# The samples' attention moved half a unit back in TensorE's order, in one layer of a hybrid decoder

## The chip, the cores and the metric

The kernel runs on one core of one Trainium2 chip. The time is the device time of one execution in microseconds (us); a change is judged by the median of several executions. The profile is that of one execution, whose times are counted from the start of its span.

## The reference

One step of a one-layer decoder is computed, in float32, for two kinds of rows at once: a prompt of 512 tokens and 8 samples of one token each, 520 columns in all. Cut to what matters:

```
h = modulate(rms_norm(x, g_pre_mix), shift_m, scale_m)
u, q, k, v, z_pool, z_att = split(h @ w_in)
y_pool = pool_mix(u_ext, pos, w_map, scale) @ w_proj_pool
# samples: 24 heads = 3 groups x 8 slots, 129 keys each, 128 of them from a cache
s = einsum('btsd,btjsd->btsj', q, kg) * HEAD_DIM ** -0.5
p = exp(s - m);  o = einsum('btsj,btjsd->btsd', p, vg) / den
o = merge_groups(outs, lses)            # 3 groups -> 8 slots of 64
y_att = o @ w_proj_att
mix = (sigmoid(z_pool) * y_pool + sigmoid(z_att) * y_att) @ w_out
x = x + gate_m * rms_norm(mix, g_post_mix)
...                                     # then a convolved, gated feed-forward
```

The new key and value caches are outputs too, so that large copies in HBM run beside the computation.

## The kernel before

Activations lie transposed in SBUF: 128 channels on the partitions, 520 columns (TC) beside each other, D = 1024 as 8 such tiles. A product with a weight matrix is cut into **units**. A full unit has 8 weight tiles of 128x128 (512 KB), loaded by SP into one of four `raw` buffers. ScalarE copies it to `w_hi` in a rounded format (L699, in its helper `split`), VectorE takes the rest, `w_lo` (L932, in its own `split`), and TensorE multiplies in `blocks` (L1335) hi by hi, hi by lo and lo by hi: 24 groups of two matmuls for each output tile, one group for each weight tile loaded. A unit's result is in one of two PSUM accumulators, and `take` waits until the one needed has been evacuated. The splits of a unit are done two units ahead.

Each engine has its own program, written out by hand in a fixed order, and they meet in semaphores. The change is in the **middle stage**, whose order is `MID`: two units `map`, eight units `pp` (the projection of the pooled branch), four units `pa` (the projection of the attention, two output tiles each, from `o_hi` and `o_lo`). The `out` units come behind it. Within a `pp` unit TensorE does four tiles, then whatever was put in the middle, then the other four.

The attention of the samples is threaded through this stage in steps:

- GpSimd multiplies cached keys by queries (L672); VectorE sums each product over the head's channels in six reductions, `sample_scores(0)` to `sample_scores(5)` (L1139, output `sall`). The last is issued in the iteration of `pp` 4, behind that iteration's weight split.
- `sample_in` (TensorE, L1609): three transposes that sort the scores so that each of the 64 pairs of sample and slot has a partition. It waits for all six reductions.
- `sample_softmax` (VectorE, L1143 to L1161, with ScalarE's exponential at L818 in the middle), which also makes `o_new`, the part of the new token.
- `sample_turn` (TensorE, L1615): three transposes of the softmax weights into PSUM; VectorE copies them to `prT` (L1192, three copies).
- `sample_values` (TensorE, L1627): 48 matmuls of `prT` with the cached values `vS`, which SP loads in six blocks (`load_v`, 1 MB each). Before `load_v(5)` SP waits for the sixth reduction.
- VectorE adds `o_new` and masks, giving `o_rows` (L1198, L1201).
- `sample_out` (TensorE, L1635): eight small matmuls that put each head of a pair of slots and each sample in its place, as columns 512 to 519 of the attention's output.
- ScalarE and VectorE write these columns as `o_hi` and `o_lo` (L829, L1209, semaphore `os_lod`).

The first attention unit, pa0, is done in quarters by `one_half` (L1344): two output tiles, each with the first 260 columns (half 0) and then the last 260 (half 1). Only half 1 has the samples' columns, so TensorE waits for `os_lod` between the halves.

On VectorE, an iteration of `pp` holds in this order: what the samples need, the product of `thp` with the accumulator (L1206, which frees it), the split of the weights two units ahead, and a reduction of scores. SP's order of transfers around here is: pp6's tile, two V blocks, pp7's tile, two V blocks, pa0's tile, V blocks 4 and 5, the tiles of pa1 to pa3, some small outputs, the tiles of `out`. With the first `out` units go the loads `ada_last` (1 MB each), the first of which waits until `sample_values` is done.

Of the kernel before, what the change touches and what calls it, by code (L numbers as in the profile page):

```python
# [8 lines left out]
ALU = mybir.AluOpType  # L9
# [90 lines left out]
def program(nc, ins, outs):  # L100
# [5 lines left out]
    with ExitStack() as ctx:  # L106
# [582 lines left out]
        def _(act):  # L689
# [108 lines left out]
            for pos, (what, m) in enumerate(MID):  # L798
# [17 lines left out]
                if (what, m) == ("pp", 5):  # L816
                    act.wait_ge(smp_max, 1)
                    act.activation(sc[0:NB * NS, :], sc[0:NB * NS, :], ACT.Exp, bias=bh_stat[0:NB * NS, 0:1], scale=1.0,  # L818
                                   accum_out=bh_stat[0:NB * NS, 1:2]).then_inc(smp_exp, 1)
# [7 lines left out]
                if (what, m) == ("pp", 7):  # L827
                    act.wait_ge(smp_summed, 1)
                    act.activation(o_hi[:, :, TP:TC], psT[:, 0:PAIRS * NB].rearrange("p (a b) -> p a b", a=PAIRS), ACT.Copy).then_inc(os_hid, 1)  # L829
# [84 lines left out]
        def _(dve):  # L914
# [256 lines left out]
            for pos, (what, m) in enumerate(MID):  # L1171
# [12 lines left out]
                if what == "pp":  # L1184
                    if m == 5:
                        sample_softmax()
                    if m == 7:
# [6 lines left out]

                        dve.wait_ge(pv_done, 1)
# [7 lines left out]

                    done(dve, u)
                    v = halves(thp[:, m, :])
                    dve.scalar_tensor_tensor(v, v, 1.0, of(("pp", m)), ALU.add, ALU.mult).then_inc(free(("pp", m)), 1)  # L1206
                    if m == 7:
                        dve.wait_ge(os_hid, 1)
                        dve.tensor_tensor(o_lo[:, :, TP:TC], psT[:, 0:PAIRS * NB].rearrange("p (a b) -> p a b", a=PAIRS),  # L1209
                                          o_hi[:, :, TP:TC].bitcast(F32), ALU.subtract).then_inc(os_lod, 1)  # L1210
                    split(N[u] + 2)
                    if m < 5:
                        sample_scores(m + 1)
                    if m == 7:
                        dve.wait_ge(ada_out, OADA)
                        gains(gg_m, 0, KT, 16, 56, 0.0)
# [111 lines left out]
        def _(pe):  # L1328
# [310 lines left out]
            for pos, (what, m) in enumerate(MID):  # L1639
# [13 lines left out]
                if what == "pp":  # L1653
# [4 lines left out]
                    if m == 5:  # L1658
                        sample_in()
                    if m == 7:  # L1660
                        sample_values()
# [6 lines left out]
                    if m == 6:  # L1668
                        sample_turn()
                    if m == 7:  # L1670
                        sample_out()
                if what == "pa":
                    if m == 0:

                        for q in range(2):
                            take(("pa", q))
                            one_half(("pa", q), slot, [(2 * kt + q, kt) for kt in range(4)], o_hi, o_lo, 0)
                        pe.wait_ge(os_lod, 1)
# [147 lines left out]
```

## Time and profile before

| | |
|---|---|
| median of 3 runs | 1068.6 us (1068.44 to 1069.54) |
| the profiled execution, its own time | 1067.55 us |
| its span | 1065.7 us |
| TensorE busy | 1023.8 us, 96% of the span |
| VectorE, ScalarE, GpSimd busy | 480.4, 401.7, 120.3 us |
| mean granted clock of TensorE | 0.975 of full speed |
| middle stage | about 469 to 571 us |

The engines are named PE (TensorE), DVE (VectorE), ACT (ScalarE), POOL (GpSimd) and SP; SPq is SP's queue of transfers, and PEld are TensorE's weight loads. L12 is line 12 of the kernel. The granted clock is 1.00 at 2.4 GHz. A row of a timeline gives the start, how long it took, engine, line, output and inputs, how many instructions it merges, and in brackets the engine's idle time before it with what ended it. Matmuls are pipelined, so that one that takes 0.40 us by its row is followed by the next after 0.24; starts are what to count by.

### The profile page before, as it was taken

How to read it: one execution, taken by the hardware profiler on the slowest of the kernel's cores; microseconds unless marked ns; L12 is line 12 of the kernel's file. 1: busy time of each engine (PE TensorE's matmuls, PEld its weight loads, DVE VectorE, ACT ScalarE, POOL GpSimd, SP SyncE). 2: the span in 40 equal slices, each digit the busy share in tenths (PEclk: the TensorE clock that was granted, in tenths of full speed). 3: DMA queues.
4: the chain of work that ended last, by engine and by line, in shares of the span. 5: the costliest groups of instructions: out<-in, count | busy, mean ns of one | idle time of the engine just before them, and what ended most of it. 6: DMA issues, size and time to landing. Idle time of an engine off the chain costs nothing.

```text
span 1065.7 us, 20398 instructions
## 1 busy us (share of the span) xinstructions
PE 1023.8 (96%) x8597; PEld 969.5 (91%) x8597; DVE 480.4 (45%) x861; ACT 401.7 (38%) x642; POOL 120.3 (11%) x165
## 2 busy tenths in 40 slices
PE   5999999999999999999899987999999999999995
PEld 3799999999999999998889965999999999999994
DVE  6533324331443143338846356556555565422214
ACT  5424422433244224432114345444545545322213
POOL 1000300040004000416512021000000000000000
PEclk8899999999999999999999997999999999999996
DMA  9966676667666876329967670566666666665302
GB/s 315 284 210 206 208 236 237 214 207 245 235 211 206 260 251 231 121 75 379 366 220 234 195 234 35 167 228 214 229 221 221 228 218 200 198 218 177 106 25 81
DMA packets 227721, 222.30 MB, mean 209 GB/s; under 512 B 6270, under 2 KB 191998, under 8 KB 226846
## 3 DMA queue, kind: packets, MB, share of 16 engines
q1 hardware_dynamic: 227545, 220.85, 62.8%
q8 instruction: 69, 1.13, 0.5%
q14 instruction: 23, 0.18, 0.0%
q10 hardware_dynamic: 84, 0.15, 0.0%
HBM read 213.56 MB, written 96.03 MB: 291 GB/s over the span
## 4 chain that ended last, share of the span: by engine, by line
PE 87%; DVE 5%; ACT 2%; DMA 2%; SPq 1%; issue 1%; POOL 1%; ACTq 0%; POOLq 0%; DVEq 0%
PE acc L1335 75%; PE psS L1507 2%; PE psT L1521 2%; DMA raw<-in_w_proj_pool 1%; PE psS L1495 1%; DMA ada_first<-in_w_ada 1%; PE psT L1535 1%; POOL ssq L638 1%; DVE w_lo L932 1%; DVE xT L1274 1%; PE psT L1555 1%; PE psS L1493 1%; PE acc L1601 1%; ACT norm_u L728 1%; PE psS L1387 1%
## 5 line engine op out<-in xcount | busy, mean ns | idle before, releaser
L1335 PE MATMUL acc<-act_hi,w_hi 128*128 128x260 f32 x1920 | 395.3, 287 | 7.4 <-DVE act_lo L1005 5.0
L1335 PE MATMUL acc<-act_hi,w_lo 128*128 128x260 f32 x1920 | 387.7, 284 | 0.0
L1335 PE MATMUL acc<-act_lo,w_hi 128*128 128x260 f32 x1920 | 387.4, 283 | 0.0
L932 DVE TENSOR_TENSOR w_lo<-raw,w_hi 128x1024 fp32r<-128x1024 f32 (+1 forms) x148 | 190.1, 1285 | 357.8 <-ACT w_hi L699 357.2
L1335 PEld LDWEIGHTS acc<-act_hi,w_hi 128*128 128x128 f32 x1920 | 297.3, 190 | 16.1 <-DVE act_lo L1005 7.8
L1335 PEld LDWEIGHTS acc<-act_hi,w_lo 128*128 128x128 f32 x1920 | 297.0, 189 | 0.0
L1335 PEld LDWEIGHTS acc<-act_lo,w_hi 128*128 128x128 f32 x1920 | 297.0, 189 | 0.0
L699 ACT ACTIVATE w_hi<-raw 128x1024 fp32r<-128x1024 f32 (+1 forms) x148 | 154.9, 1046 | 180.3 <-PE acc L1335 170.1
L1335 PE MATMUL acc<-g_hi,w_hi 128*128 128x260 f32 x352 | 71.0, 283 | 0.0
L1335 PE MATMUL acc<-g_hi,w_lo 128*128 128x260 f32 x352 | 70.8, 282 | 0.0
L1335 PE MATMUL acc<-g_lo,w_hi 128*128 128x260 f32 x352 | 70.6, 282 | 0.0
L882 ACT ACTIVATE he<-acc 128x520 f32<-128x520 f32 x44 | 26.7, 607 | 87.6 <-PE acc L1335 87.6
L1335 PEld LDWEIGHTS acc<-g_lo,w_hi 128*128 128x128 f32 x352 | 54.3, 188 | 0.0
L1335 PEld LDWEIGHTS acc<-g_hi,w_hi 128*128 128x128 f32 x352 | 54.2, 188 | 0.0
L1335 PEld LDWEIGHTS acc<-g_hi,w_lo 128*128 128x128 f32 x352 | 54.2, 188 | 0.0
L1310 DVE TENSOR_TENSOR cv<-cv,hsc 128x8 f32<-128x8 f32 x44 | 7.7, 174 | 87.9 <-ACT cv L883 87.9
L755 ACT ACTIVATE S<-S,stat 128x256 f32<-128x256 f32 (+1 forms) x64 | 31.2, 489 | 41.7 <-DVE stat L1057 41.7
L645 POOL COPY u_tail<-uT 128x46 f32<-128x46 f32 x4 | 0.9, 225 | 395.4 <-ACT uT L781 395.4
L686 POOL COPY hu_tail<-he 128x10 f32<-128x10 f32 x44 | 9.1, 207 | 261.3 <-ACT cv L883 261.3
L778 ACT ACTIVATE qkvT<-acc 128x520 f32<-128x520 f32 x16 | 17.4, 1086 | 56.1 <-PE acc L1335 56.1
L883 ACT ACTIVATE cv<-acc,vec 128x520 f32<-128x520 f32 x44 | 34.3, 780 | 0.0
L1313 DVE SCALAR_TENSOR_TENSOR cv<-he,vec,cv 128x512 f32<-128x512 f32 x44 | 33.1, 752 | 1.6
(248 smaller groups left out, 952.1 us busy)
## 6 DMA issues: line engine op xcount, KB each, us to landing
out_k_sample<-in_cache_k_w SPq DMA_DIRECT2D x89, 368.0 KB
out_v_sample<-in_cache_v_w SPq DMA_DIRECT2D x89, 368.0 KB
raw<-in_w_in SPq DMA_DIRECT2D x60, 512.0 KB, 6.3
raw<-in_w_up SPq DMA_DIRECT2D x44, 512.0 KB, 5.6
ada_last<-in_w_ada SPq DMA_DIRECT2D x12, 1024.0 KB, 8.2
ada_first<-in_w_ada SPq DMA_DIRECT2D x9, 1024.0 KB, 9.6
raw<-in_w_down SPq DMA_DIRECT2D x16, 512.0 KB, 4.8
out_k_sample<-in_cache_k_w SPq DMA_DIRECT2D x16, 511.0 KB
```

The lines of the kernel that those rows point to most:

```text
L638: pool.tensor_tensor(ssq[:, :], ssq[:, :], sq[:, k % 2, :], ALU.add).then_inc(ssqd, 1)
L699: act.activation(w_hi[PLACE[n]][:, 0:unit_cols(n)], raw[:, n % RAW, 0:unit_cols(n)], ACT.Copy).then_inc(hi_ready, 1)
L728: act.activation(u[:, k, 0:TP], u[:, k, 0:TP], ACT.Identity, bias=mod[:, shift0 + k, PROMPT:MC], scale=a[:, k, PROMPT:MC]).then_inc(u_read ...
L755: act.activation(S[:, t % 2, h, lo:], S[:, t % 2, h, lo:], ACT.Exp, bias=stat[:, j // 4, 0, h, j % 4:j % 4 + 1], scale=-1.0, accum_out=sta ...
L778: act.activation(by_class(qkvT[:, k, :]), in_time(of(s)), ACT.Copy, scale=scale).then_inc(free(s), 1)
L882: act.activation(halves(he[half][m][:, 2:2 + TC]), of(s), ACT.Copy)
L883: act.activation(halves(cv[half][m][:, :]), of(s), ACT.Identity, bias=bc, scale=w2).then_inc(free(s), 1)
L932: dve.tensor_tensor(w_lo[PLACE[n]][:, 0:cols], raw[:, n % RAW, 0:cols], w_hi[PLACE[n]][:, 0:cols].bitcast(F32), ALU.subtract).then_inc(lo_ ...
L1313: dve.scalar_tensor_tensor(c[:, 0:TP], h[:, 0:TP], w0, c[:, 0:TP], ALU.mult, ALU.add).then_inc(taps, 1)
L1335: ins_ = pe.matmul(acc[b][:, half, 0:HALF], w, x[:, t, half * HALF:(half + 1) * HALF], start=first and i == 0 and j == 0, stop=last and i ...
L1507: ins_ = pe.matmul(psO[64 * h:64 * h + 64, :], v, PT[:, t % 2, (2 * h + c) * P:(2 * h + c + 1) * P], start=c == (1 if i == 0 else 0), stop ...
L1521: ins_ = pe.transpose(blk(psT[:, 0:512], 2 * h + c), blk(S[:, (t - 1) % 2, h, :], c), ident[:, :])
```

## The change

Five steps move, each by about half a unit of TensorE:

| step | before | after |
|---|---|---|
| `sample_in` | middle of pp5 | middle of pp6 |
| softmax (VectorE, ScalarE) | ahead of pp5's evacuation | ahead of pp6's evacuation |
| `sample_turn` | end of pp6 | middle of pp7 |
| `sample_values` | middle of pp7 | end of pp7 |
| `sample_out` | end of pp7 | in pa0, behind its first quarter |

On VectorE the wait for the values, `o_rows` and the samples' `o_lo` now come behind pp7's product and the split of pa1's weights instead of ahead of them. On ScalarE the samples' `o_hi` moves from pp7 to the start of pa0. Nothing is added or removed, and SP's program is the same.

```diff
-                if (what, m) == ("pp", 5):
+                if (what, m) == ("pp", 6):
                     act.wait_ge(smp_max, 1)
                     act.activation(sc[0:NB * NS, :], sc[0:NB * NS, :], ACT.Exp, ...
...
-                if (what, m) == ("pp", 7):
+                if (what, m) == ("pa", 0):
                     act.wait_ge(smp_summed, 1)
                     act.activation(o_hi[:, :, TP:TC], psT[:, 0:PAIRS * NB]...
...
                 if what == "pp":                                   # VectorE
-                    if m == 5:
+                    if m == 6:
                         sample_softmax()
                     if m == 7:
                         dve.wait_ge(smp_turned, 1)
...
                         ins_.then_inc(pr_ready, 1)
 
+                    done(dve, u)
+                    v = halves(thp[:, m, :])
+                    dve.scalar_tensor_tensor(v, v, 1.0, of(("pp", m)), ALU.add, ALU.mult)...
+                    split(N[u] + 2)
+                    if m < 5:
+                        sample_scores(m + 1)
+                    if m == 7:
                         dve.wait_ge(pv_done, 1)
...
                                           ALU.mult).then_inc(o_rowed, 1)
-
-                    done(dve, u)
-                    v = halves(thp[:, m, :])
-                    dve.scalar_tensor_tensor(v, v, 1.0, of(("pp", m)), ALU.add, ALU.mult)...
-                    if m == 7:
                         dve.wait_ge(os_hid, 1)
                         dve.tensor_tensor(o_lo[:, :, TP:TC], ...
-                    split(N[u] + 2)
-                    if m < 5:
-                        sample_scores(m + 1)
-                    if m == 7:
                         dve.wait_ge(ada_out, OADA)
...
                     blocks(("pp", m), slot, [(i, i) for i in range(KT // 2)], ...)   # TensorE
-                    if m == 5:
+                    if m == 6:
                         sample_in()
                     if m == 7:
-                        sample_values()
+                        sample_turn()
                     blocks(("pp", m), slot, [(i, i) for i in range(KT // 2, KT)], ...)
...
-                    if m == 6:
-                        sample_turn()
                     if m == 7:
-                        sample_out()
+                        sample_values()
                 if what == "pa":
                     if m == 0:
 
                         for q in range(2):
                             take(("pa", q))
                             one_half(("pa", q), slot, ..., o_hi, o_lo, 0)
+                            if q == 0:
+                                sample_out()
                         pe.wait_ge(os_lod, 1)
```

## Rows read from the trace of the kernel before

**Rows 1.** The page, busy time of each engine over the span.
```profile
PE 1023.8 (96%) x8597; PEld 969.5 (91%) x8597; DVE 480.4 (45%) x861; ACT 401.7 (38%) x642; POOL 120.3 (11%) x165
```

**Rows 2.** TensorE's waits over the whole span: total us, times, longest.
```profile
PE psT L1609 <- DVE sall L1139: 4.0, 1, 4.0
...
PE acc L1335 <- DVE w_lo L932: 2.0, 2, 1.1
```

**Rows 3.** Timeline of TensorE, pp5 to the start of pa1: start, us.
```profile
520.21 0.41 PE L1335 MATMUL acc<-act_hi,w_lo 128*128 128x260 f32 x2
524.57 0.52 PE L1609 MATMUL psT<-ident,sall 128*64 128x128 f32 x3 [3.95 <-DVE sall L1139]
524.85 0.49 PE L1335 MATMUL acc<-act_hi,w_hi 128*128 128x260 f32 x2
...
529.34 0.40 PE L1335 MATMUL acc<-act_hi,w_hi 128*128 128x260 f32 x2
...
538.58 5.36 PE L1627 MATMUL psT<-cached,prT 128*32 128x512 f32 x48
543.87 0.51 PE L1335 MATMUL acc<-act_hi,w_hi 128*128 128x260 f32 x2
...
547.65 0.36 PE L1344 MATMUL acc<-o_hi,w_hi 128*128 128x260 f32 x1
...
549.19 0.29 PE L1344 MATMUL acc<-o_hi,w_hi 128*128 128x260 f32 x1
...
553.50 0.41 PE L1335 MATMUL acc<-o_hi,w_hi 128*128 128x260 f32 x2
```

**Rows 4.** Windows: us, busy time of each engine, PEclk, DMA share, GB/s.
```profile
525.00:527.00 2.00, 2.00 (x13) 2.00 (x13) 1.57 (x5) 0.30 (x1) 0.00 (x0) 0.58 1.05 402
...
531.00:550.00 19.00, 19.00 (x162) 14.83 (x161) 6.45 (x11) 2.21 (x3) 0.00 (x0) 1.00 0.56 199
540.00:550.00 10.00, 10.00 (x91) 7.07 (x84) 3.19 (x5) 1.15 (x2) 0.00 (x0) 1.00 0.16 47
570.00:600.00 30.00, 28.88 (x246) 28.49 (x246) 12.03 (x14) 10.30 (x15) 2.72 (x2) 1.00 0.93 306
...
645.00:650.00 5.00, 4.35 (x21) 4.35 (x22) 0.85 (x5) 0.21 (x1) 0.60 (x1) 0.50 0.00 0
```

**Rows 5.** Timeline of VectorE, from the last reduction of scores to pa0.
```profile
522.25 2.27 DVE L1139 TENSOR_REDUCE sall<-cached 128x32 f32<-128x2048 f32 x1
524.59 0.11 DVE L1143 MEMSET o_new<- 64x64 f32 x1
...
528.37 0.59 DVE L1161 SCALAR_TENSOR_TENSOR o_new<-bh,sc,o_new 64x64 f32<-64x64 f32 x2
529.54 0.70 DVE L1206 SCALAR_TENSOR_TENSOR thp<-thp,acc 128x520 f32<-128x520 f32 x1 [0.58 <-PE acc L1335]
530.71 1.23 DVE L932 TENSOR_TENSOR w_lo<-raw,w_hi 128x1024 fp32r<-128x1024 f32 x1 [0.48 <-ACT w_hi L699]
...
544.73 0.69 DVE L1201 TENSOR_TENSOR o_rows<-o_rows,own_head 128x512 f32<-128x512 f32 x1
...
548.12 0.19 DVE L1209 TENSOR_TENSOR o_lo<-psT,o_hi 128x32 fp32r<-128x32 f32 x1 [0.39 <-ACT o_hi L829]
```

**Rows 6.** SP's issues of pp7, V block 5, pa1; us from issue to landing.
```profile
513.56 2.17 SPq L347 DMA_DIRECT2D raw<-in_w_proj_pool  x1
raw<-in_w_proj_pool SPq DMA_DIRECT2D x1, 512.0 KB, 9.9
...
524.55 0.72 SPq L449 DMA_DIRECT2D cached<-in_cache_v_w  x1
cached<-in_cache_v_w SPq DMA_DIRECT2D x1, 1024.0 KB, 10.7
...
525.31 3.68 SPq L347 DMA_DIRECT2D raw<-in_w_proj_att  x2
raw<-in_w_proj_att SPq DMA_DIRECT2D x1, 512.0 KB, 11.3
```

More of the change, by code:

```diff
@@ L1193, in _ @@
                         ins_.then_inc(pr_ready, 1)
+                    done(dve, u)
+                    v = halves(thp[:, m, :])
+                    dve.scalar_tensor_tensor(v, v, 1.0, of(("pp", m)), ALU.add, ALU.mult).then_inc(free(("pp", m)), 1)
+                    split(N[u] + 2)
+                    if m < 5:
+                        sample_scores(m + 1)
+                    if m == 7:
                         dve.wait_ge(pv_done, 1)
@@ L1202, in _ @@
                                           ALU.mult).then_inc(o_rowed, 1)
-                    done(dve, u)
-                    v = halves(thp[:, m, :])
-                    dve.scalar_tensor_tensor(v, v, 1.0, of(("pp", m)), ALU.add, ALU.mult).then_inc(free(("pp", m)), 1)
-                    if m == 7:
                         dve.wait_ge(os_hid, 1)
```

## The prediction

> **What bounds the kernel now.** I read the page first: TensorE is busy for 96% of the span [rows 1], so what can be won is idle time of TensorE and time at its lower clock. The list of its waits over the whole span gives the places. One of the single ones is the wait for `sall` at L1609, 4.0 us [rows 2]; it stands in the middle of unit pp5, where `sample_in` sorts the scores of the samples. Nothing else in the middle stage costs TensorE over 1.2 us. Then I read TensorE's timeline around that wait [rows 3]. A group is one weight tile with two matmuls; groups start 0.24 us apart (that is 24 groups, a whole unit, in 5.76 us). The last group ahead of the sort starts at 520.21, so the second half of pp5 could have begun at 520.45. The sort starts at 524.57 and the second half at 524.85. The timeline also shows a second loss: from 524.85 to 529.34 the 12 groups of the second half take 4.49 us where 12 x 0.24 = 2.88 are due. The windows say why: the granted clock is 0.58 from 525 to 527 and 1.00 from 531 on [rows 4], so TensorE ran mostly at the lower of its two levels (1.2 instead of 2.4 GHz) for some 3 us after it had stood for 4.
>
> What TensorE waited for is VectorE, not a transfer: its last reduction of the scores (`sample_scores(5)`) runs from 522.25 for 2.27 us to 524.52 [rows 5], with no idle time in front of it. Nothing in the change moves that end.
>
> **The change, part by part.**
>
> *The sort of the scores, from the middle of pp5 to the middle of pp6.* pp5 then runs through: its second half ends at 520.45 + 2.88 = 523.33, where pp6 started at 529.34 [rows 3]: 6.01 us earlier. That is 4.12 us of standing, 1.61 us of lower clock and the sort itself, 0.28 us (524.57 to 524.85), which is not removed but comes back in pp6. Is pp6 able to start at 523.33? Its weights were split on VectorE ahead of the last reduction, so before 522.25 [rows 5]. The middle of pp6 is at 523.33 + 2.88 = 526.21, 1.7 us behind the reduction's end at 524.52: no wait. Term so far: 6.01 - 0.28 = **5.73 us**.
>
> *VectorE's softmax, from before pp5's evacuation to before pp6's.* From 524.52 VectorE now takes pp5's product with `thp` (0.70 us, as at 529.54) and the split of pp7's weights (1.23 us [rows 5]) first. The split needs pp7's tile: issued at 513.56, landed 9.9 us later, 523.5 [rows 6]; ScalarE's copy of it comes first, and from the end of a unit to the start of VectorE's split that was 1.37 us (529.34 to 530.71 [rows 3, 5]), so the split can start at 524.9. VectorE gets to it at 525.2. So the softmax begins near 526.5 instead of 524.59 and takes the same 4.4 us (524.59 to 528.96, its second row ending 0.59 us after 528.37 [rows 5]): `o_new` is ready at 530.9. TensorE wants it for the turn of the weights (`sample_turn`), which moves from the end of pp6 to the middle of pp7. That is at 523.33 + 5.76 + 0.28 + 2.88 = 532.25: slack 1.3 us. Behind the softmax on VectorE are pp6's product and the split of pa0's weights, done by 530.9 + 0.7 + 1.23 = 532.8; pa0 wants them at 541. ScalarE's exponential moves with the softmax and has nothing urgent behind it. Cost 0, and if that cover were gone, each us that the softmax is late beyond 1.3 is a us of TensorE.
>
> *The values (`sample_values`, 48 matmuls), from the middle of pp7 to its end.* They ran from 538.58 to 543.87 [rows 3], 9.24 us behind pp6's start. Now 12 groups and the sort lie in between as well: 523.33 + 9.24 + 2.88 + 0.28 = 535.73. Two conditions. The weights in `prT` are there at 532.25 + 0.4 + three copies, about 533.4. The last block of V (`load_v(5)`) is issued on SP only after the last reduction, at 524.55, and landed 10.7 us later: 535.25 [rows 6]. That leaves 0.5 us. The 10.7 is counted from the start of the issue; from its end (0.72 us later) the landing would be at 535.97, a wait of 0.25. SP's order of issue is not touched, and all that stands ahead of this block in the queue is gated by VectorE and GpSimd work that the change leaves alone. I take 0; the bounds are 0 and 2.4 us, the latter if the block landed only when pa1's and pa2's tiles behind it had landed too: pa1's landed at 536.6 [rows 6], 1.35 us behind V, and pa2's, of the same size and next in the queue, should be as much later, 538.0.
>
> The Trainium skill ("DMA: Bandwidth & Descriptors", section "Queues, rings and completion order") states that completion is not first in, first out for one issuing engine. The landings of rows 6 do come in the order of issue; by that section they need not. By my reading the sum loses nothing, by the Trainium skill's rule up to the 2.4 us of the upper bound.
>
> *What follows the values on VectorE.* pp7's product and the split of pa1's weights now stand ahead of the wait for the values. pa1's tile landed at 525.31 + 11.3 = 536.6 [rows 6]; ScalarE's copy (1.37 with its handoff) and VectorE's split (1.23) add 2.6, so 539.2, and the values end at 541.0. Hidden by 1.8 us.
>
> *The sum over the values (`sample_out`), from the end of pp7 to behind the first quarter of pa0.* VectorE needs from the end of the values to the end of `o_rows` 543.87 to 545.42 = 1.55 us [rows 3, 5]; in that time twelve groups of pp7 (2.9 us) used to cover it, now it is one quarter of pa0, 547.65 to 549.19 = 1.54 us [rows 3]. The cover is just used up: I charge 0.1 us (bounds 0 and 0.3, the gaps between engines being 0.02 to 0.09 us in these rows). Then `os_lod` (`o_lo` at 548.12 plus 0.19, so 0.66 us behind the start of pa0, which is the end of the sum) is covered by the second quarter, 1.5 us.
>
> *SP.* The weight tiles of pa3 and of the first `out` units are gated by splits that now come about 5 us earlier; they queue behind the V block, not ahead of it. From 540 to 550 the DMA engines are busy for 0.16 [rows 4], so there is room. The big `ada_last` loads wait for the values, for pa3 and for the merged tiles, all of which come earlier by the same amount. The next waits of TensorE (1.1 us at the third `out` unit, within the 2.0 of [rows 2]) hang on a unit's end, and move along.
>
> **The sum.** 6.01 - 0.28 - 0.1 = **5.6 us**. The profiled execution took 1067.55 us with a span of 1065.7, so it would become 1061.9 with a span of 1060.1; its time lies 1.05 us under the median of the runs, 1068.6. Against that median: 1068.6 - 5.6 = **1063.0 us**.
>
> **Rivals.**
>
> 1. *V lands late.* For: only 0.5 us of slack where there were 3.3 (535.25 against 538.58), with the DMA engines at 1.05 from 525 to 527 [rows 4]. Against: the landings in order of issue, and nothing new ahead of the block. A wait of 0.3 to 2.4 us gives 1063.3 to 1065.4. The Trainium skill's rule on completion would show itself this way.
> 2. *The softmax comes late.* The softmax now hangs behind pp7's split; if that tile lands 2.2 us later (525.7, counted from the end of its issue, which took 2.17 [rows 6]), the split runs from 527.0, `o_new` comes at about 532.7 and TensorE waits 0.4; with up to 0.6 more for a slower step in that chain, 1063.4 to 1064.0.
> 3. *No change.* The time is given back at a later point that is fixed by transfers. For: from 570 to 600 weight tiles and the 1 MB `ada_last` blocks keep the DMA engines at 0.93 [rows 4]. Against: each issue there waits on a unit, not on the clock on the wall. It would give about 1068.6.
> 4. *Slower: the lower clock under the values.* If TensorE must wait for V right ahead of 48 matmuls with 32 columns of weights, the clock may fall there and stay low for all 5.29 us of them and the first quarter of pa0 (1.54): at half the clock 6.8 us more. Together with a wait of 2.4 us that is 9.2 against 5.6 won: 3.6 slower, 1072.2. It decides from a wait of about 0.9 us on (0.9 + 6.8 = 5.6 + 2.1), if the clock falls at all. Against: behind the 1.1 us wait on `w_lo` [rows 2], which lies in 570 to 600, the clock stays at 1.00, and so it does in 531 to 550, where the values run now [rows 4].
>
> **How the numbers follow.** Chances: forecast 0.73, rival 1 0.12, rival 2 0.06, rival 3 0.06, rival 4 0.03. The median of a few runs can tell a difference from none at about 0.2%, 2.1 us. The forecast and rivals 1 and 2 are faster by more than that (at most 1065.4 against 1066.5); of their 0.91 I take off 0.01 for mishaps together. Faster 0.90, same 0.07, slower 0.03. The range: below, the forecast's sum without the 0.1 and with the shown runs' spread of 1.1 us, since shifting the rest by 5.6 us can change how long the low clocks of the later stages last (645 to 650 stands at 0.50 [rows 4]): 1061.5, rounded down to 1061.3. Above, rival 1's 1065.4 and part of that spread: 1066.2. Rivals 3 and 4, 0.09 together, stay out.
>
> **What would show it.** In the trace of after: no wait for `sall` in the list of waits; clock 1.00 throughout 520 to 545; pp6's first group near 523.3; the sort near 526.2, the turn near 532.3, the values from 535.7 to 541.0 with no idle time before them; pa1's first group at 547.9 instead of 553.50 [rows 3]; from there all rows shifted by 5.6 us. The prediction fails if the values wait for a transfer for over a us, if `sample_turn` waits for VectorE, or if the waits behind 570 grow.

## The result and the profile after

| | before | after |
|---|---|---|
| median of the runs | 1068.91 us (1068.44 to 1069.54, 4 runs) | 1060.55 us (1059.02 to 1061.38, 4 runs) |
| profiled execution | 1067.55 us | 1060.58 us |
| its span, its mean clock | 1065.7 us, 0.975 | 1058.8 us, 0.978 |

The ratio is 0.9919 with a 95% interval of 0.9902 to 0.9936. The change is worth 8.4 us by the medians where 5.6 were predicted; 1060.55 lies just below the range, which began at 1061.3. Four executions on each side are few: repeats in experiments 3 and 4 give 7.6 and 7.7 us by the medians.

The page of the kernel after, busy times, answers to [rows 1], and TensorE's list of waits over the whole span to [rows 2]:

```profile
PE 1020.3 (96%) x8597; PEld 968.0 (91%) x8597; DVE 480.4 (45%) x861; ACT 401.8 (38%) x642; POOL 120.1 (11%) x165
...
PE acc L1333 <- DVE w_lo L932: 2.0, 2, 1.1
```

The wait for `sall` is gone, the one for `w_lo` is the same, and the instruction counts are the same. The lines are two lower than before from the softmax on (L1335 is L1333 now). TensorE's timeline after, from pp6 to the start of pa1, beside [rows 3]:

```profile
522.91 0.40 PE L1333 MATMUL acc<-act_hi,w_hi 128*128 128x260 f32 x2
...
525.80 0.49 PE L1607 MATMUL psT<-ident,sall 128*64 128x128 f32 x3
...
532.01 0.40 PE L1613 MATMUL psT<-ident,sc 64*128 64x64 f32 x3
...
535.40 5.36 PE L1625 MATMUL psT<-cached,prT 128*32 128x512 f32 x48
540.69 0.39 PE L1342 MATMUL acc<-o_hi,w_hi 128*128 128x260 f32 x1
...
542.39 1.03 PE L1633 MATMUL psT<-own_sample,o_rows 128*128 128x8 f32 x8
...
547.66 0.41 PE L1333 MATMUL acc<-o_hi,w_hi 128*128 128x260 f32 x2
```

Every row stands within 0.45 us of its forecast: pp6 at 522.91 (forecast 523.3), the sort at 525.80 (526.2), the turn at 532.01 (532.3), the values at 535.40 (535.7), pa1 at 547.66 (547.9). No row waits. Most of the small offset was there already: VectorE's last reduction ends at 524.14 instead of 524.52. Its timeline, beside [rows 5]:

```profile
521.87 2.27 DVE L1139 TENSOR_REDUCE sall<-cached 128x32 f32<-128x2048 f32 x1
524.67 1.21 DVE L932 TENSOR_TENSOR w_lo<-raw,w_hi 128x1024 fp32r<-128x1024 f32 x1
...
529.73 0.59 DVE L1161 SCALAR_TENSOR_TENSOR o_new<-bh,sc,o_new 64x64 f32<-64x64 f32 x2
...
541.55 0.69 DVE L1208 TENSOR_TENSOR o_rows<-o_rows,own_head 128x512 f32<-128x512 f32 x1
```

So `o_new` is ready at 530.3 and wanted at 532.01 (slack 1.7, forecast 1.3), and that `o_rows` ends at 542.24, with the sum following at 542.39, at the end of the first quarter of pa0. The windows say what became of the clock, beside [rows 4]:

```profile
520.00:545.00 25.00, 25.00 (x210) 20.64 (x209) 15.08 (x26) 4.09 (x6) 1.66 (x2) 1.00 1.04 371
540.00:550.00 10.00, 10.00 (x84) 9.14 (x77) 3.88 (x7) 1.64 (x3) 2.62 (x2) 1.00 0.99 314
```

TensorE is busy all the time at 1.00, as forecast. The DMA share between 540 and 550 is 0.99 where it was 0.16. SP's issues say why, beside [rows 6]:

```profile
524.17 0.37 SPq L449 DMA_DIRECT2D cached<-in_cache_v_w  x1
cached<-in_cache_v_w SPq DMA_DIRECT2D x1, 1024.0 KB, 10.5
...
540.82 2.05 SPq L372 DMA_DIRECT2D ada_last<-in_w_ada  x2
```

The last block of V landed at 534.67, 0.7 us ahead of its first use. The big `ada_last` loads, gated by the values, start at 540.82; before, they started at 550.78, so they come 10 us earlier, where the prediction had them earlier by the same amount as the values and the merged tiles. TensorE has no wait on a transfer there that the kernel before lacks.

**Where the other 3 us come from.** I cut both profiles at the same events and compare the lengths (us):

| stretch | before | after | difference |
|---|---|---|---|
| start to the last reduction of scores | 522.25 | 521.87 | 0.38 |
| to ScalarE's first copy of a merged tile | 32.14 | 26.68 | 5.46 |
| to the first `spread` (L1415 before, L1413 after) | 72.96 | 71.47 | 1.49 |
| to the last late fold | 38.08 | 37.57 | 0.51 |
| (378.8 us, equal) then from the last sum to the end | 21.41 | 22.37 | -0.96 |

The second row is the predicted 5.6. The third has no term in the prediction's sum. TensorE's timeline at the late `ada` product, before and then after:

```profile
622.81 1.28 PE L1409 MATMUL acc<-ones,ssq 128*128 128x1 f32 x10 [1.24 <-DVE ssq L1248]
624.01 3.41 PE L1720 MATMUL acc<-ada_last,siluT 128*32 128x256 f32 x32
```

```profile
616.95 1.28 PE L1407 MATMUL acc<-ones,ssq 128*128 128x1 f32 x10 [1.23 <-DVE ssq L1246]
618.15 1.93 PE L1718 MATMUL acc<-ada_last,siluT 128*32 128x256 f32 x32
```

And the windows over that product, before and then after:

```profile
624.00:628.00 4.00, 4.00 (x37) 2.02 (x37) 0.85 (x5) 0.21 (x1) 0.00 (x0) 0.57 1.09 384
```

```profile
617.00:621.00 4.00, 4.00 (x52) 3.06 (x52) 1.03 (x6) 1.01 (x2) 0.00 (x0) 1.00 1.10 387
```

The same 32 matmuls behind the same wait of 1.2 us ran mostly at 1.2 GHz before (3.41 us, clock 0.57) and at 2.4 GHz after (1.93 us, 1.00): 1.48 us. The differences sum to 6.9, the difference of the spans. The remaining 1.4 of 8.4 is that the profiled execution before was 1.4 us below its median, while the one after was at its median.

Much of what one execution differs from the next by lies far ahead of the change. ScalarE's fifth copy of a weight tile starts at 58.65 us before and 58.26 after, but at 56.41 in one profile of experiment 1 (rest_only) and at 60.47 in one of experiment 4 (early_b). The windows over the first 60 us, rest_only and then early_b:

```profile
0.00:60.00 60.00, 46.33 (x406) 37.64 (x407) 34.05 (x83) 28.23 (x40) 4.23 (x30) 0.94 0.93 291
```

```profile
0.00:60.00 60.00, 45.36 (x366) 37.10 (x367) 31.68 (x80) 26.95 (x39) 4.23 (x30) 0.83 0.92 285
```

The granted clock is 0.94 in the one and 0.83 in the other, and those 4.06 us are still the difference at 460 us. A comparison of two whole times has this in it; one of later stretches has not.

### The profile page after: what moved, and what is told of

Same layout as the page of the kernel before. It is cut to its first block, busy times and chain, and to the rows that moved or that the text cites. A ratio compares the mean times of both kernels' runs of the same rounds, so it can differ in the third digit from the quotient of the medians.

```text
span 1058.8 us, 20397 instructions
## 1 busy us (share of the span) xinstructions
PE 1020.3 (96%) x8597; PEld 968.0 (91%) x8597; DVE 480.4 (45%) x861; ACT 401.8 (38%) x642; POOL 120.1 (11%) x165
## 4 chain that ended last, share of the span: by engine, by line
PE 90%; DVE 4%; ACT 2%; SPq 1%; issue 1%; DMA 1%; POOL 0%; ACTq 0%; DVEq 0%; POOLq 0%
PE acc L1333 78%; PE psS L1505 2%; PE psT L1519 2%; PE psS L1493 1%; DMA ada_first<-in_w_ada 1%; PE psT L1533 1%; DVE xT L1272 1%; PE psT L1553 1%; PE psS L1491 1%; PE acc L1599 1%; ACT norm_u L728 1%; PE acc L1342 1%; PE psS L1385 1%; DVE ffn L1270 1%; PE psT L1625 0%
## 5 line engine op out<-in xcount | busy, mean ns | idle before, releaser
L1333 PE MATMUL acc<-act_hi,w_hi 128*128 128x260 f32 x1920 | 394.3, 287 | 8.5 <-DVE act_lo L1005 6.2
L1333 PE MATMUL acc<-act_hi,w_lo 128*128 128x260 f32 x1920 | 387.2, 283 | 0.0
L1333 PE MATMUL acc<-act_lo,w_hi 128*128 128x260 f32 x1920 | 387.0, 283 | 0.0
L1333 PEld LDWEIGHTS acc<-act_hi,w_hi 128*128 128x128 f32 x1920 | 296.2, 189 | 15.9 <-DVE act_lo L1005 8.0
L1333 PEld LDWEIGHTS acc<-act_hi,w_lo 128*128 128x128 f32 x1920 | 296.6, 189 | 0.0
L1333 PEld LDWEIGHTS acc<-act_lo,w_hi 128*128 128x128 f32 x1920 | 296.5, 189 | 0.0
L1333 PE MATMUL acc<-g_hi,w_hi 128*128 128x260 f32 x352 | 71.0, 283 | 0.0
L1333 PE MATMUL acc<-g_hi,w_lo 128*128 128x260 f32 x352 | 70.8, 282 | 0.0
L1333 PE MATMUL acc<-g_lo,w_hi 128*128 128x260 f32 x352 | 70.6, 282 | 0.0
L1333 PEld LDWEIGHTS acc<-g_lo,w_hi 128*128 128x128 f32 x352 | 54.3, 188 | 0.0
L1333 PEld LDWEIGHTS acc<-g_hi,w_hi 128*128 128x128 f32 x352 | 54.2, 188 | 0.0
L1333 PEld LDWEIGHTS acc<-g_hi,w_lo 128*128 128x128 f32 x352 | 54.2, 188 | 0.0
```

The source lines that it names most:

```text
L1333: ins_ = pe.matmul(acc[b][:, half, 0:HALF], w, x[:, t, half * HALF:(half + 1) * HALF], start=first and i == 0 and j == 0, stop=last and i ...
```

## The experiments

"Before" beside a number is the median of the kernel before, measured beside it. The ratio counts every execution, the median only the middle ones; where a few executions are far off, the two say different things.

**1. The two halves of the change.** b_again is the kernel before once more. sort_only moves the sort, softmax and exponential alone (from the kernel before, in all three places):

```diff
-if (what, m) == ("pp", 5):     # ScalarE; also VectorE's and TensorE's  if m == 5
+if (what, m) == ("pp", 6):     #                                        if m == 6
```

rest_only is the changed kernel with those three back at 5: only the turn, the values and the sum are moved.

> The kernel before, unchanged, in five rounds of its own. Theory 1 (the mechanism was as predicted, 5.7 us, and the rest of the 8.4 us is low clock of TensorE in later stages that happens to be shorter): the executions differ among themselves by about 1 us, longer ones with a lower mean granted clock, and the mean clock is 0.974 to 0.976 where the changed kernel's executions had 0.978 to 0.980, that is 3 to 5 us less of full clock. Theory 2 (the profiled execution of before was a lucky one and the wait on the scores is longer in most others): the same times, 1068 to 1070, but a mean clock that is not lower where the time is longer. Ratio 1.000 either way.

> Only the sort of the scores and the softmax move from pp5 to pp6; the turn stays at the end of pp6, the values in the middle of pp7, the sum at its end. By the prediction's steps pp5's wait (5.73 us with its low clock) goes, the turn waits for the softmax until 530.9 where it would like to start at 529.4 (1.5 us), and the values, due at 534.2, wait for the last V block until 535.3 (1.1 us): net gain 3.1 us, 1065.5 us. Theory 1 allows 1 to 2 us more or less by the clock of later stages. A rival that holds that the last V block lands earlier when TensorE doesn't stand has no wait at the values and a gain of 4.2 us.

> The sort and the softmax stay in pp5; the turn, the values and the sum move as in the change. The wait of 4 us on the scores stays. Prediction's steps: no gain and 0.1 us lost at the sum, 1068.9 us, within 0.5 us plus what the clock of later stages does. A rival by which half of the gain comes from the later place of the values or the sum (evacuation of pp7 and the split of pa1 ahead of them) gives 2 to 3 us here.

Measured, before 1068.58 us: b_again 1067.67 (0.9999, 0.9989 to 1.0010); sort_only 1064.79 (1060.78 to 1067.05), 0.9957 (0.9940 to 0.9973); rest_only 1068.31 (1066.44 to 1069.98), 0.9997 (0.9988 to 1.0005). The last part alone is worth nothing and the first alone about half. In sort_only's profile the middle stage, from the last reduction to the first merged tile, lasts 29.11 us, 3.0 less than before, where the expectation's steps gave 3.1. TensorE's waits of sort_only say where the other half is:

```profile
PE psT L1627 <- DMA cached<-in_cache_v_w: 1.3, 1, 1.3
PE psT L1615 <- DVE o_new L1161: 1.2, 1, 1.2
```

With the sort moved alone, the turn at the end of pp6 and the values in pp7 come before their inputs, by 1.2 and 1.3 us. So the turn's and the values' places cost nothing in the kernel before only because the wait for `sall` covered them, and the last block of V really is the next thing that is late. In rest_only the wait for `sall` is whole:

```profile
PE psT L1607 <- DVE sall L1139: 4.0, 1, 4.0
```

Its middle stage is 1.0 us longer than before (33.17), mostly since the low clock behind the wait lasted longer: the 12 groups there take 5.04 us instead of 4.49.

**2. Is part of the loss the clock?** filler is the kernel before with 33 spare matmuls in the place where TensorE waits for `sall`; their result is not used:

```diff
                     if m == 5:
+                        for f in range(FILL):      # 33
+                            pe.matmul(psS[...HALF], blk(mix_hi[:, 0, :], 0), mix_lo[:, 1, 0:HALF], ...)
                         sample_in()
```

> The kernel before with 33 matmuls of 260 columns ahead of the sort in pp5, written to a part of PSUM that nobody reads: 33 x 0.12 = 4.0 us of work where TensorE stood for 4.1. The end of the wait does not move; only the low clock behind it should go. Theory 1: pp6 starts 1.6 us earlier, gain 1.6 us plus or minus 1.7 by the later stages. Theory 2 (the low clock behind the wait costs more in most executions than in the profiled one): a gain of 3 us and more. If the fall of the clock had another cause than standing: no gain.

Measured: 1065.97 us, before 1068.58; 0.9988 (0.9968 to 1.0008). Its twelve executions lie in two groups, eight at 1061.4 to 1068.4 and four at 1070.8 to 1072.7, so the whole times show no gain that is clear of noise. The window over pp5's wait, for filler and then for rest_only (the order of the kernel before at this place), says more:

```profile
519.00:526.00 7.00, 6.94 (x59) 6.74 (x58) 6.88 (x8) 0.28 (x1) 3.47 (x2) 1.00 1.07 395
```

```profile
519.00:528.00 9.00, 5.41 (x26) 5.34 (x27) 6.96 (x13) 0.71 (x2) 1.05 (x2) 0.62 1.06 405
```

With TensorE kept busy the clock stays at 1.00, and the middle stage lasts 30.65 us instead of 32.14. The 1.5 us between them is the predicted term for the lower clock, 1.61, measured by itself. The other 4.1 is the standing. A second profile of the same kernel, filler_look, gives 30.62.

> One more profile of the kernel before with 33 spare matmuls in pp5's wait, whose times fell into two groups (1061 to 1066 and 1070 to 1073). Theory 1: the slower group has low clock in a stretch where TensorE is the bound, at the start of the up units or of the whole kernel, 10 us or more of it. A rival: the slower group has later transfers and a new wait in the middle stage.

filler_look measured 1066.85 us, so that neither profile met the slower group; its cause was not seen.

**3. Does the time at which the later stages run decide whether the clock falls ahead of the first `spread`?** a_again is the changed kernel once more; delay2, delay3 and delay5 put 17, 28 and 46 spare matmuls ahead of pa2 in it, 0.12 us each:

```diff
                 if what == "pa":
+                    if m == 2:
+                        for f in range(FILL):      # 17, 28 or 46
+                            pe.matmul(psS[...HALF], blk(o_hi[:, 0, :], 0), o_lo[:, 1, 0:HALF], ...)
```

> The changed kernel, unchanged, in five rounds of its own beside the kernel before on one chip. The kernel before spreads over 4.4 us in 29 executions, so four executions of the changed one don't settle the size. Theory 2 (the gain is the predicted 5.6 us, up to 6.3 with an average fall of the clock, and four executions were lucky): a median of 1062.3 to 1063. Theory 1 (a lasting extra gain, since the waits of the later stages now stand otherwise to the stretches of low clock): 1060 to 1061, mean clock 0.979 again.

> The changed kernel with 17 matmuls of 260 columns (2.04 us of work) ahead of the attention unit pa2, written to a part of PSUM that nobody reads; all that follows comes 2 us later. Theory 2 (times add up in a straight line): 2.0 us more than the changed kernel. Theory 1 (where the later waits fall relative to the stretches of low clock decides): 3.5 to 5 us more, with a low-clock stretch on the late ada matmuls ahead of the first spread, which the changed kernel's profile lacks.

> The same with 28 matmuls, 3.4 us of work. Theory 2: 3.4 us more than the changed kernel, thus 1.4 more than the delay of 2 us. Theory 1: 3 to 3.8 us more than the changed kernel, so no slower than the delay of 2 us or even faster than it, and no low clock ahead of the first spread.

> The same with 46 matmuls, 5.5 us of work: the stages behind pa2 then come as late as in the kernel before. Theory 2: 5.5 us more than the changed kernel, about 1066. Theory 1: the later stages lose to the clock as in the kernel before, 7 to 8 us more than the changed kernel, about 1068, and the same durations of the stages behind as in the kernel before (73.0 us from the first merged tile to the first spread, against 71.5).

Measured, before 1068.98 us:

| | median, us | ratio to before |
|---|---|---|
| a_again | 1061.41 (1058.9 to 1068.19) | 0.9948 (0.9922 to 0.9973) |
| delay2 | 1065.03 (1060.1 to 1067.35) | 0.9959 (0.9945 to 0.9974) |
| delay3 | 1066.31 (1062.48 to 1074.19) | 0.9989 (0.9967 to 1.0011) |
| delay5 | 1067.83 (1065.31 to 1073.39) | 1.0004 (0.9989 to 1.0019) |

Two of a_again's seven executions, at 1067.8 and 1068.2, pull its ratio down to a gain of 5.6 us, where its median gives 7.6. The delays cost 3.6, 4.9 and 6.4 us by the medians and 1.6, 4.5 and 5.9 by the means, so the whole times do not tell the two theories apart. The profiles show more. The late `ada` product in the three, in that order:

```profile
621.29 3.39 PE L1723 MATMUL acc<-ada_last,siluT 128*32 128x256 f32 x32
```

```profile
622.80 3.30 PE L1723 MATMUL acc<-ada_last,siluT 128*32 128x256 f32 x32
```

```profile
624.31 1.93 PE L1723 MATMUL acc<-ada_last,siluT 128*32 128x256 f32 x32
```

The stretch before the first `spread` grew by 3.48, 4.93 and 5.50 us against a_again's 71.48. delay2 and delay3 cost their 2.0 and 3.4 us of matmuls and another 1.5 for a fall of the clock; delay5 costs its 5.5 alone. So the lower clock is not bound to how late the product runs: it was low at 621.29 and 622.80 and full at 624.31, with one profile of each. What can be said is how often it fell. Of the kernels whose sort stands in pp5 I have five profiles, rest_only with its later steps moved and two with pp5's tile moved (experiment 4): in before, b_again, rest_only and early_b the product takes 3.36 to 3.49 us, in late_b 1.94. Of the changed order there are five as well, two of them with pp5's tile moved: in after, a_again and a_look it takes 1.93 to 1.94 us, in late_a 2.76, so that the clock fell in a part of it, and in early_a it takes this:

```profile
618.91 3.58 PE L1718 MATMUL acc<-ada_last,siluT 128*32 128x256 f32 x32
```

And this is the row of late_b, in the old order, where it did not fall:

```profile
625.79 1.94 PE L1720 MATMUL acc<-ada_last,siluT 128*32 128x256 f32 x32
```

With four of five against two of five, whether the order has a part in it is not shown.

> One more profile of the changed kernel. Both theories: no wait on the scores, 26.7 us from the last reduction of scores to the first merged tile. Theory 1: whether the clock falls ahead of the first spread differs among executions, and that is 1.5 us. If this execution is one of those near 1068, its profile shows where the 7 us are.

a_look measured 1060.12 us. Of the old order's profiles, before, b_again and early_b have neither a moved turn nor the long split of experiment 4; of the changed order's, after, a_again, a_look and early_a. Over these three and four, the mean length of the middle stage is 32.37 and 26.71 us (5.7), of the next stretch 72.96 and 71.88 (1.1), and of the one after 38.08 and 37.70 (0.4): 7.1 us together. The middle stage is sure to 0.1 us in the changed order (26.68 to 26.73) and varies in the old one with the low clock behind the wait (32.14, 32.17, 32.78). The 1.1 hangs on the count above; with late_a and late_b in it, it would be 0.6.

**4. Two executions of a_again were at 1067.8 and 1068.2, the rest at 1058.9 to 1061.9. What do they meet?** In the trace, GpSimd's last multiplication of the scores' block and VectorE's split of pp5's weights start within half a microsecond of each other. After (GpSimd, then VectorE):

```profile
515.26 5.60 POOL L672 TENSOR_TENSOR cached<-cached,qB 128x2048 f32<-128x2048 f32 x1
...
514.77 1.61 DVE L932 TENSOR_TENSOR w_lo<-raw,w_hi 128x1024 fp32r<-128x1024 f32 x1 [1.15 <-ACT w_hi L699]
```

I moved pp5's tile in SP's program, one way and the other, in both kernels: early issues it ahead of the last Q and K blocks, late behind the gather of `bh`, so that VectorE's split should come sooner or later.

```diff
# early                         # late
+proj_pool(5)                   -proj_pool(5)
 load_q(5); load_k(5)            sp.dma_start(bh[...], scratch...)
-proj_pool(5)                   +proj_pool(5)
```

> The changed kernel; on SP the weight tile of pp5 is issued two 1 MB loads earlier (ahead of the last queries and keys). It should land near 510.5 instead of 513.5, and VectorE's split of it starts well before GpSimd's last multiplication. Theory 3 (in a part of the executions that split starts just after GpSimd's multiplication and then takes 5.6 us instead of 1.9; the kernel before hides most of it under the wait on the scores, the changed one pays it all, 5 to 7 us): the same main group at 1060 to 1061, but no execution near 1068. If the slow group has another cause: as with the changed kernel, 2 in 11 near 1068.

> The kernel before with the same edit on SP. Theory 3: its times stay where they are, 1067 to 1069, since the wait on the scores ends no earlier; the difference to the changed kernel with that edit is the middle stage's 5.5 us, plus 0.5 to 2 for low clock behind it and in the later stages: 6 to 7.5 us.

> The changed kernel with pp5's weight tile issued behind the small gather of the samples' rows, so that it lands about 2 us later, always behind the start of GpSimd's last multiplication. Theory 3: all executions are in the slow group, 1066 to 1069; the profile shows the split of pp5 with 4 to 5.6 us, a wait of TensorE on it of 3 to 4 us, the last reduction of scores 2.5 to 3 us later and low clock behind the wait. If the split's start does not matter: 1061 to 1063.

> The kernel before with pp5's weight tile issued behind the small gather, as in late_a. Theory 3: here the late split (5.3 us) moves the last reduction of scores by 2.5 to 3 us, and TensorE waits 3.6 us on the split and under 1 on the scores instead of 4.0: only 1 to 3 us more than the kernel before, 1069.5 to 1071.5, where the same edit cost the changed kernel 6.2 in the median. If the kernel before pays it in full as well: 1074 and more.

| | changed order (a) | old order (b) |
|---|---|---|
| early | 1060.99 (1059.72 to 1062.63), 0.9925 (0.9911 to 0.9938) | 1068.72 (1067.13 to 1071.71), 1.0000 (0.9989 to 1.0011) |
| late | 1067.24 (1059.8 to 1069.07), 0.9972 (0.9954 to 0.9991) | 1069.24 (1067.06 to 1072.19), 1.0002 (0.9992 to 1.0011) |

Before was 1068.63 us beside the first three and 1068.83 beside late_b. With the split early, none of six executions of the changed kernel is near 1068. That is weak evidence: where two in twelve are long, six in a row without one come up in one case of three. With the split late, nine of late_a's twelve executions stand at 1065.7 to 1069 and three at 1059.8 to 1062.5. The trace of late_a (GpSimd, VectorE, and the row of TensorE's waits):

```profile
515.16 4.54 POOL L672 TENSOR_TENSOR cached<-cached,qB 128x2048 f32<-128x2048 f32 x1
...
515.47 5.32 DVE L932 TENSOR_TENSOR w_lo<-raw,w_hi 128x1024 fp32r<-128x1024 f32 x1 [1.95 <-ACT w_hi L699]
520.71 2.27 DVE L1139 TENSOR_REDUCE sall<-cached 128x32 f32<-128x2048 f32 x1
...
PE acc L1333 <- DVE w_lo L932: 4.6, 2, 3.6
```

The split that starts 0.3 us behind the start of GpSimd's last multiplication lasts 5.32 us. It ends 1.1 us behind that multiplication (519.70), and 1.21 is what a split takes with GpSimd idle (the row at 524.67). The same holds for the short ones. The split at 514.77 in after starts before the last multiplication, but within the one before it, which ends at 515.3, and it ends 1.1 us behind that one, at 516.38. The last multiplication, which starts at 515.26, then takes 5.60 us instead of 4.54. In all 19 profiles together 92 weight splits of this part (485 to 530 us) start while GpSimd multiplies. Every one ends 1.08 or 1.09 us behind the multiplication in which it started. The 18 that start with GpSimd idle take 1.21 to 1.23 us. So what decides is on which side of the last multiplication's start the split of pp5 comes, and in after it was 0.5 us.

In late_a TensorE waits 3.6 us at pp5 for the long split. The old order meets the same thing in late_b, and its median moves by 0.4 us only (1069.24 against 1068.83), because there TensorE would stand for `sall` in that unit anyway. These are late_b's waits:

```profile
PE acc L1335 <- DVE w_lo L932: 4.8, 2, 3.6
PE psT L1609 <- DVE sall L1139: 1.5, 1, 1.5
```

3.6 + 1.5 of standing has taken the place of 4.0. From ScalarE's copy of a weight tile at 462 us to the first merged tile the profiles take 92.2 us before and 93.8 in late_b, but 86.7 after and 92.2 in late_a: the long split costs 1.6 us in the old order and 5.4 in the changed one. The Trainium skill ("GPSIMD Engine Reference", section "Specifications") says that GpSimd's SBUF interfaces are shared with VectorE and contended for by VectorE instructions with two SBUF inputs, as this split is. The trace agrees: 5.32 us against 1.21. That a_again's two long executions met this was not seen, since neither was profiled. Their size speaks for it, about 7 us above the rest where late_a's median is 6.3 above early_a's.

**5. Keeping TensorE busy in the late waits.** warm_a (from the changed kernel) and warm_b (from the kernel before) put spare matmuls, whose result is not used, where TensorE waits from the first late sum on and at the end. early_warm is warm_a with the early tile of experiment 4.

```diff
+def warm(n, bank=1):
+    for _ in range(n):
+        pe.matmul(acc[1][:, bank, 0:HALF], blk(w, 0), w[:, 0:HALF], start=True, stop=True)
+warm(5)                 # ahead of the first late sum
 sum_columns()
...
+warm(17)                # then late_fold(3); warm(32) ahead of the second sum
...
+warm(4 if k else 8, 0)  # each k of the first "up" unit
...
+warm(7)                 # last sum; warm(10) spread(4); warm(17), then 2 per k, the turns at the end
```

> The changed kernel with the same spare matmuls in the later stages. Theory 1: the difference to the kernel before with the spare matmuls is that of the middle stage alone, 5.5 to 6.3 us, and not 8; it is also the fastest version so far, 1059 to 1061. Theory 2: as the changed kernel, 1061, and 8 us under its partner.

> The kernel before, with spare matmuls of 260 columns (written to a PSUM bank that is free just then) in TensorE's waits from 620 to 665 and from 1042 on, so that TensorE doesn't stand there; the wait of pp5 is left as it is. Theory 1 (what the change wins beyond 5.6 us, and most of the spread of the times, comes from low clock in the later stages): the low clock from 624 to 655 goes or shrinks, the spread falls under 3 us, and the median comes down by 2 to 4 us to 1065 to 1067. Theory 2: the later low clock costs nothing, as TensorE mostly waits there: within 1 us of before.

> The changed kernel with both: pp5's tile earlier and the spare matmuls in the later waits. Theory 3: 1055 to 1057.5 in all executions, the fastest version, with the smallest spread.

Measured: warm_a 1056.65 us (1054.91 to 1057.26), 0.9882 (0.9868 to 0.9897); warm_b 1063.73 (1061.68 to 1066.49), 0.9950 (0.9934 to 0.9967), both beside a before of 1069.43; early_warm 1057.02 (1056.18 to 1059.62), 0.9895 (0.9879 to 0.9911), beside 1068.63. warm_a and warm_b are both lower than either theory had them, and warm_b's spread is 4.8 us where theory 1 had it under 3. The mean clock is 0.9925 (warm_a) and 0.988 (warm_b) where the kernel before has 0.975. warm_a is the fastest version, and early_warm is not measurably different: two of its five executions, at 1059.1 and 1059.6, miss the 1055 to 1057.5 expected of all. The one at 1059.1 was profiled, and has a wait of 3.0 us on another unit's split, where the other profiles of this order that I read have 0.9 to 1.4:

```profile
499.48 0.51 PE L1333 MATMUL acc<-act_hi,w_hi 128*128 128x260 f32 x2 [3.00 <-DVE w_lo L932]
```

The early tile did not keep TensorE from a long wait on a split. The windows over the late stages, after and then warm_a:

```profile
630.00:660.00 30.00, 21.70 (x162) 16.44 (x162) 20.20 (x44) 18.27 (x28) 7.00 (x6) 0.83 0.17 62
...
1036.00:1058.00 22.00, 13.61 (x55) 9.28 (x55) 12.66 (x25) 6.91 (x11) 0.00 (x0) 0.53 0.28 98
```

```profile
630.00:660.00 30.00, 28.20 (x237) 24.77 (x230) 20.39 (x44) 17.79 (x27) 5.82 (x5) 0.94 0.13 47
...
1034.00:1053.00 19.00, 12.20 (x89) 9.89 (x88) 12.32 (x24) 6.00 (x10) 0.00 (x0) 1.00 0.32 113
```

At the end of the kernel the clock is 1.00 instead of 0.53, and the stretch from the last sum to the end is 19.99 us instead of 22.37. With the late clock held up in both orders, the two medians still differ by 7.1 us, where the theory that the surplus is late clock gave 5.5 to 6.3. So this pair does not bear that theory out. The two profiled executions differ by 9.6 us of span: 2.3 in the first 60 us, 2.4 more up to the last reduction of scores, 3.87 in the middle stage (30.62 against 26.75) and 1.0 in the rest. The 2.4 is the long split of experiment 4 (5.64 us), which warm_b's profile met. How many of the executions behind the medians met it isn't known, so the pair can't isolate the middle stage.

## Why the prediction was right in place and short in size

- **The sum's main term, 6.01 - 0.28.** Right. The middle stage is 5.46 us shorter in the two profiles and 5.7 over three and four; 5.6 was predicted. Its inner split (standing 4.1, clock 1.6, sort 0.3 coming back) is borne out by filler, which won the clock part alone in the profile of the middle stage: 1.5.
- **"`o_new` is ready at 530.9 ... slack 1.3 us."** Right: 530.3 and 1.7. Rival 2 did not occur.
- **"That leaves 0.5 us" for V.** Right: 0.7. Rival 1 did not occur, and neither did rival 4, which needed it. (The upper bound of this wait, 2.4, doesn't follow from its own rows: 538.0 - 535.73 is 2.3. Nothing hangs on it.) sort_only shows the wait of 1.3 us that follows once the values run half a unit sooner.
- **"The cover is just used up: I charge 0.1 us."** The sum starts 0.15 us behind the end of `o_rows`, more than the gaps of 0.02 to 0.09 that the prediction had read and within its bounds of 0 to 0.3, and TensorE shows no wait there.
- **"No change": the time given back at a transfer.** It did not happen, though the `ada_last` loads moved by 10 us and not by the same amount as the rest.
- **The failed step: "with the shown runs' spread of 1.1 us, since shifting the rest by 5.6 us can change how long the low clocks of the later stages last", and its pair "from there all rows shifted by 5.6 us".** The prediction knew the mechanism, gave it 0 in the sum and 1.1 us in the range, and let every row behind the middle stage shift alike. They did not. In the two profiles the stretch ahead of the first `spread` gave 1.49 us more and the next one 0.51, and the end took 0.96 back: 1.0 us net. The fall of the clock on the late `ada` product costs 1.5 us where it happens, in four of the five profiles with the sort in pp5 and, wholly or in part, in two of five with it in pp6. The mean of the profiles is 7.1 us, against 7.7 between the medians of early_a and early_b (1068.72 - 1060.99).
- **The size of the spread.** 1.1 us was that of three runs. The kernel before, in 29 executions, spreads over 4.4 us (1066.24 to 1070.62), and up to 4.1 us of that kind lie in the first 60 us, where the clock was 0.83 to 0.94. The profiled execution of before lay 1.05 us under the median that the prediction started from, the one of after at its own; the sum carried the 1.05 over unchanged. The lower end of the range doesn't follow from its words either: 1068.6 - 5.7 - 1.1 is 1061.8, not 1061.5. Even the lower number printed, 1061.3, had no room for 1060.55.
- **Luck.** Four executions of the changed kernel met none of its long ones. All twelve on record, a_again and a_look with them, have a median of 1060.8 us and a mean of 1061.8, and a_again's median of 1061.41 by itself lies inside the predicted range.

What stays open: why the clock falls on that product in one execution and not in another, and whether the old order makes it likelier. The rows in front of it are alike (a wait of 1.2 us, then ten matmuls with one column). The position in time is not enough by itself, since delays of 2.0 and 3.4 us had the fall and one of 5.5 us had not, with one profile each. Open too is where the surplus over 5.6 us in the medians comes from, beyond the 1.5 us or so that the profiles place: with the late clock held up in both orders it did not shrink.

## What to carry to other kernels

A step that waits in the middle of a unit is moved back by as much as its input is late, and everything behind it has to move along: the first half alone (sort_only) won half. Price the next input that is late, here a V block with 0.7 us of slack, from the old trace's rows; that was accurate to 0.5 us. But behind it there are places at which TensorE nearly stands, and whether the clock falls at one was worth 1.5 us here. Count them, take the spread from many executions rather than three, compare stretches of the profiles and not only whole times, and try spare matmuls in such waits: they won 4.0 us here in the changed order (early_a to early_warm) and 5.7 in the old one (before to warm_b).

## What the runs showed of the hardware

- A VectorE `tensor_tensor` with two SBUF inputs that started within one of GpSimd's `tensor_tensor` multiplications ended 1.08 or 1.09 us behind it, in 92 of 92 rows, whether it had started 0.3 us into it (5.3 us, late_a) or nearly at its end (1.6 us, after). With GpSimd idle it took 1.21 to 1.23 us. A GpSimd multiplication that started in the last part of a waiting split took 5.6 us instead of 4.54. In early_a the split starts 3.8 us into the fifth multiplication (510.43 to 516.0):

```profile
514.27 2.84 DVE L932 TENSOR_TENSOR w_lo<-raw,w_hi 128x1024 fp32r<-128x1024 f32 x1
```

  Half a microsecond in the landing of one tile can thus decide over 5.4 us of the kernel in the changed order, and over 1.6 in the old one, where the wait for the scores covers most of it. Removing a wait exposed this second one.
- 33 spare matmuls in a wait of 4 us held TensorE's clock at 1.00 over a stretch where it was 0.62 without them (filler, rest_only). In the late waits the spare matmuls lowered the medians by 4.0 and 5.7 us, so that any price of the extra work is less than what they won.
- DMA blocks landed in the order of issue in all rows read here. The last 1 MB block of V took 10.7 us from its issue before and 10.5 after, though pa3's tile was issued behind it at 528.28 instead of 531.97.
